# A mixture of experts reads its rows in quarters: 32x32 block transposes on VectorE in place of TensorE's, down weights four neighbouring rows to a partition, gate and up weights at a step of four

## What is computed

```python
def hier_moe(x, norm_g, w_rg, w_re, w_gate, w_up, w_down):
    u = rms_norm(x, norm_g)
    ...
    expert_id = g_sel * EXPERTS_PER_GROUP + top_i
    dense_w = jnp.sum(jax.nn.one_hot(expert_id, N_EXPERTS, dtype=jnp.float32) * gate[..., None], axis=-2)
    h = jax.nn.silu(jnp.einsum('ntd,edf->ntef', u, w_gate)) * jnp.einsum('ntd,edf->ntef', u, w_up)
    h = h * dense_w[..., None].astype(h.dtype)
    return jnp.einsum('ntef,efd->ntd', h, w_down)
```

## Time and profile before

| | |
|---|---|
| median of 3 runs | 1395.42 us (1392.59 to 1399.41) |
| profiled execution | 1393.3 us, its span 1391.3 us |
| PE busy | 1283.8 us, 92% |
| PEld busy | 975.2 us, 70% |
| DVE busy | 516.1 us, 37% |
| ACT busy | 308.4 us, 22% |
| POOL busy | 168.5 us, 12% |
| mean TensorE clock granted | 0.949 of full |
| moved by DMA | 437.00 MB, mean 314 GB/s |

### The profile page before, as it was taken

The page is one execution under the profiler, slowest core; times in us unless marked ns, Lnnn a source line. Parts: engine busy times, 40 slices in busy tenths (PEclk is TensorE's granted clock), DMA queues, the critical chain, the costliest instruction groups (busy, mean ns, idle before and its releaser), DMA issues.

```text
span 1391.3 us, 36243 instructions
## 1 busy us (share of the span) xinstructions
PE 1283.8 (92%) x15268; PEld 975.2 (70%) x15268; DVE 516.1 (37%) x1323; ACT 308.4 (22%) x767; POOL 168.5 (12%) x202
## 2 busy tenths in 40 slices
PE   5979999999986999999999898999997899999996
PEld 5869999999634766667675454545445899999983
DVE  3640000000176545564647566663026200000005
ACT  2200011111142131314144453534101011111000
POOL 4110000010202021212122111210000000000003
PEclk9869999999997999999999899999987899999999
DMA  8959999999898879897979898984264699999976
GB/s 283 369 183 372 382 391 388 393 399 363 295 362 285 278 249 364 274 384 260 384 256 356 263 359 261 345 301 182 93 255 149 245 384 390 391 389 389 390 295 212
DMA packets 147222, 437.00 MB, mean 314 GB/s; under 512 B 20711, under 2 KB 51304, under 8 KB 138270
## 3 DMA queue, kind: packets, MB, share of 16 engines
q1 hardware_dynamic: 99494, 367.58, 71.2%
q10 hardware_dynamic: 37296, 38.09, 8.4%
q0 software_dynamic: 10320, 29.79, 6.7%
HBM read 406.32 MB, written 29.44 MB: 313 GB/s over the span
## 4 chain that ended last, share of the span: by engine, by line
PE 66%; issue 12%; DVE 8%; ACT 6%; DMA 4%; SPq 2%; ACTq 1%; POOL 1%; DVEq 0%; POOLq 0%
PE PS L1102 12%; PE PS L1106 12%; PE PS L1355 8%; PE PS L1134 6%; PE PS L1492 6%; PE PS L1139 6%; PE PS L1024 3%; PE PS L1395 3%; PE PS L1433 2%; DVE KV L2433 2%; PE PS L1456 1%; PE PS L1016 1%; DVE PS L2483 1%; ACT W L1968 1%; DMA KV<-in_cache_k 1%
## 5 line engine op out<-in xcount | busy, mean ns | idle before, releaser
L1106 PE MATMUL PS<-W,KV 128*32 128x128 f32 x3072 | 345.8, 275 | 0.0
L1102 PE MATMUL PS<-W,KV 128*32 128x384 f32 x3072 | 342.6, 492 | 3.2 <-DVE KV L2054 3.2
L1106 PEld LDWEIGHTS PS<-W,KV 128*32 128x32 f32 x3072 | 338.1, 111 | 2.2
L2294 DVE TENSOR_TENSOR KV<-KV,PS 128x384 f32<-128x384 f32 x32 | 17.7, 554 | 483.2 <-PE PS L1120 426.7
L1355 PE MATMUL PS<-W 128*128 128x256 f32 x768 | 178.8, 387 | 0.7 <-ACT KV L1764 0.7
L1355 PEld LDWEIGHTS PS<-W 128*128 128x128 f32 x768 | 144.6, 193 | 30.3 <-issue 7.9
L1134 PE MATMUL PS<-W,KV 128*32 128x384 f32 x1440 | 162.2, 488 | 0.0
L1139 PE MATMUL PS<-W,KV 128*32 128x256 f32 x960 | 162.2, 327 | 0.0
L2433 DVE STREAM_TRANSPOSE KV<-KV 128x1024 f32<-128x1024 f32 x128 | 155.5, 1229 | 7.3 <-DMA KV<-in_cache_k 7.2
L1102 PEld LDWEIGHTS PS<-W,KV 128*32 128x32 f32 x3072 | 150.9, 110 | 4.5 <-DVE KV L2054 4.1
L1139 PEld LDWEIGHTS PS<-W,KV 128*32 128x32 f32 x960 | 95.6, 109 | 14.4
(11 more groups left out here) (305 smaller groups left out, 1478.8 us busy)
## 6 DMA issues: line engine op xcount, KB each, us to landing
W<-in_w_gate SPq DMA_DIRECT2D x32, 2048.0 KB
W<-in_w_up SPq DMA_DIRECT2D x32, 2048.0 KB, 15.1
W<-in_w_down SPq DMA_DIRECT2D x32, 2048.0 KB, 13.3
KV<-in_cache_k SPq DMA_DIRECT2D x256, 256.0 KB, 5.5
W<-in_cache_v SPq DMA_DIRECT2D x128, 512.0 KB, 8.1
yd<-KV ACTq DMA_DIRECT2D x30, 288.0 KB, 7.6
W<-in_w_kvf SPq DMA_DIRECT2D x4, 2048.0 KB, 18.3
W<-in_w_kvf ACTq DMA_DIRECT2D x8, 1024.0 KB, 7.8
```

The lines of the kernel that those rows point to most:

```text
L1102: pe.matmul(PS[32 * q:32 * q + 32, bank, 0:WIDE], x, w[:, k, 0:WIDE], start=(k == 0), stop=(k == KC - 1), tile_position=(0, 32 * q), skip_ ...
L1106: mm = pe.matmul(PS[CAP:P, bank, P * q:P * q + P], x, w[:, k, WIDE:FF], start=(k == 0 and q == 0), stop=(k == KC - 1), tile_position=(0, C ...
```

## The change

1. XS is also seen as rows of 256 floats (XS4), four to a row. The table IDX becomes 128 x 48: for each group q of 32 rows, partition 32a + i has 4 x (row i of the group) + a. An expert's gather is three indirect DMAs (one per q) of 128 quarter rows of 1 KB.
2. To make this come out right, `in_quarters` writes the normalised rows to XS with each quarter permuted, reading them with a step of eight floats.
3. VectorE transposes the gathered 128 x 768 in blocks of 32 x 32 into XQ[j] and multiplies it by the gains in place, three instructions. There are two such buffers, and VectorE works two experts ahead (`xt(e + 2)` behind `hidden(e)`). Expert 0 is done quarter by quarter (`xt_first`), as its three gathers land. `x_tr` is gone.
4. TensorE's order becomes gate(e), h_tr(e-1), up(e), down(e-1), and up now waits for hidden(e-1) itself (h_ready), because xt_ready no longer implies it.
5. A down weight arrives as one run of 16 KB per partition, its rows 4p to 4p + 3. The hidden columns must then come out by residues, so `product` reads the gate and up weights with a step of four: columns of residue 0, 1, 2 in the wide matmuls, of residue 3 in the narrow ones.

```diff
-            return A["w_down"][l, e].rearrange("(f p) n -> p f n", f=FC)
+            return A["w_down"][l, e].rearrange("(p f) n -> p (f n)", f=FC)
...
+        XS4 = XS.rearrange("r (a f) -> (r a) f", a=4)
+        XQ = [a[:, 0:Q4 * 2 * P] for a in (V8[:, 4, :], V4[:, :])]
+        XTQ = [a.rearrange("p (q k n) -> p q k n", q=Q4, k=KC) for a in XQ]
...
-                    after(pool, sem("xt_tr"), e - 1 + l * NE)
+                    after(pool, sem("xg_read"), e - 1 + l * NE)
...
-                    pool.indirect_dma_start(out=XG[j][0:CAP, :], out_offset=None, in_=XS,
-                                            in_offset=bass.IndirectOffsetOnAxis(ap=idc[0:CAP, j:j + 1], axis=0))\
-                        .then_inc(sem(f"xg_in_{j}"), 16)
+                    for q in range(Q4):
+                        pool.indirect_dma_start(out=XG[j][:, 2 * P * q:2 * P * q + 2 * P], out_offset=None, in_=XS4,
+                                                in_offset=bass.IndirectOffsetOnAxis(ap=idc[:, Q4 * j + q:Q4 * j + q + 1], axis=0))\
+                            .then_inc(sem(f"xg_in_{j}"), 16)
...
-                def x_tr(e, j):
-
-                    k = 8 * e + 16 - 8 * j
-                    pe.wait_ge(sem(f"xg_in_{j}"), k + l * (8 * NE))
-                    after(pe, sem("xt_ready"), e + l * NE)
-                    transposes(XG[j], 0, CAP, KC).then_inc(sem("xt_tr"), 1)
...
-                    w = W[:, slot, :].rearrange("p (k n) -> p k n", k=KC)
+                    w = W[:, slot, :].rearrange("p (k n f) -> p k f n", k=KC, f=FC)
                     for k in range(KC):
                         for q in range(Q4):
-                            x = XT[:, k, 32 * q:32 * q + 32]
-                            pe.matmul(PS[32 * q:32 * q + 32, bank, 0:WIDE], x, w[:, k, 0:WIDE], start=(k == 0),
+                            x = XTQ[j][:, q, k, :]
+                            pe.matmul(PS[32 * q:32 * q + 32, bank, 0:WIDE], x, w[:, k, 0:FC - 1, :], start=(k == 0),
                                       stop=(k == KC - 1), tile_position=(0, 32 * q), skip_group_check=True)
...
-                        product(3, 3 * j + 1, count, "up")
+                        after(pe, sem("h_ready"), e + l * NE)
+                        product(3, 3 * j + 1, count, "up", j)
...
                     halves(e, j, 0)
-                    halves(e, j, 1)
                     if not first:
                         h_tr(e - 1)
-                    x_tr(e + 1, 1 - j)
+                    halves(e, j, 1)
...
+            def in_quarters(t, out):
+
+                r = ROWS[t]
+                return dve.tensor_scalar(out[0:r, :].rearrange("p (a k n) -> p a k n", a=4, k=KC),
+                                         H[0:r, t, :].rearrange("p (a n k) -> p a k n", a=4, k=KC), rs[0:r, t:t + 1], None, ALU.mult)
...
-                dve.tensor_copy(IDX[:, :], PS[:, 7, 2 * P:2 * P + NE]).then_inc(sem("routed"), 1)
+                table = IDX[:, :].rearrange("p (q e) -> p q e", q=Q4)
+                for q in range(Q4):
+                    for a in range(4):
+                        ins = dve.tensor_scalar(table[32 * a:32 * a + 32, q], PS[32 * q:32 * q + 32, 7, 2 * P:2 * P + NE], 4.0, float(a),
+                                                ALU.mult, ALU.add)
+                    ins.then_inc(sem("routed"), 1)
...
-                def xt(e):
-                    dve.wait_ge(sem("xt_tr"), e + 1 + l * NE)
-                    gained(XT, 0, l, CAP).then_inc(sem("xt_ready"), 1)
...
+                def xt(e, j):
+                    dve.wait_ge(sem(f"xg_in_{j}"), 24 * e + 32 - 8 * j + l * (24 * NE - 16 + 16 * j))
+                    after(dve, sem("up_done"), e - 1 + l * NE)
+                    dve.transpose(XQ[j], XG[j][:, 0:Q4 * 2 * P]).then_inc(sem("xg_read"), 1)
+                    dve.wait_ge(sem("xg_read"), e + 1 + l * NE)
+                    x = XQ[j].rearrange("p (q k n) -> p q k n", q=Q4, k=KC)
+                    for q in range(Q4):
+                        g = gains[:, l, :].rearrange("p (k a) -> p k a", a=1).to_broadcast([P, KC, 32])
+                        ins = dve.tensor_tensor(x[:, q], x[:, q], g, ALU.mult)
+                    ins.then_inc(sem("xt_ready"), 1)
```

More of the change, by code:

```diff
@@ L1149, in halves @@
                         after(pe, sem("silu_done"), e + l * NE)
-                        product(2, 3 * j, count, "gate")
+                        product(2, 3 * j, count, "gate", j)
                     else:
-                        product(3, 3 * j + 1, count, "up")
+                        after(pe, sem("h_ready"), e + l * NE)
+                        product(3, 3 * j + 1, count, "up", j)
                 def expert(e, j):
@@ L1182, in down_last @@
                     mm.then_inc(sem("down_done"), 1)
-                x_tr(0, 0)
                 expert(0, 0)
@@ L1207, in moe @@
                             pe.wait_ge(sem(f"g_xg{l}"), 16 * (n + 1))
-                            transposes(XG[0], 0, P, KC).then_inc(sem(f"g_step{l}"), 1)
+                            for k in range(KC):
+                                for a in range(4):
+                                    at = 2 * P * a + 32 * k
+                                    mm = pe.matmul(PS[32 * a:32 * a + 32, k // 4, (k % 4) * P:(k % 4) * P + P], XG[0][:, at:at + 32], ident,
+                                                   start=True, stop=True, tile_position=(0, 32 * a), skip_group_check=True)
+                            mm.then_inc(sem(f"g_step{l}"), 1)
                             pe.wait_ge(sem(f"g_step{l}"), 9 * n + 2)
@@ L2032, in norm @@
                 norm_scale(phase, t)
+                if phase in ("r0", "r1"):
+                    return in_quarters(t, out)
                 if gain is None:
@@ L2302, in moe @@
                 dve.tensor_copy(ONTO[4], PS[0:CAP, 4, FC * CAP:FC * CAP + 64]).then_inc(sem("onto_step"), 1)
-                with dve.Fori(1, NE - 1) as e:
-                    hidden(e)
-                    xt(e + 1)
+                with dve.Fori(1, NE - 3, 2) as e:
+                    for j in range(2):
+                        hidden(e + j)
+                        xt(e + j + 2, 1 - j)
+                hidden(NE - 3)
+                xt(NE - 1, 1)
+                hidden(NE - 2)
                 dve.wait_ge(sem("np_ready"), 1 + l * 1)
```

71 lines of the change are left out of this document (44 added, 27 removed).

## The result

The changed kernel takes 1719.88 us (median of 4 runs, 1716.05 to 1726.23) where the kernel before takes 1394.01 us (1391.37 to 1399.41): 1.234 times as long, 95% interval 1.230 to 1.238. I had forecast 1383 us. The loss, 326 us, is the third rival's, and larger than I had priced it.

The account below looks back on a forecast made before the run. DMA queues, about 18.1 us per expert, were taken as the bound hidden by buffer lead: per stage -10.1 slack, -1.0 idle, +2.9 start, +2.0 loads = -6.2 us; two stages -12.4 us, 1383 us; range 1368 to 1406 us.

Parts of the forecast that it names:

- third rival: Gate and up products: four streams stepping on one read path stretch them; at double time about 1660 us; chance 0.18.
- The strided read: Gate and up weights read at a step of four floats: no cost, judged by a stationary-column load with step eight.
- to spare beside the loads: TensorE's spare time per expert against the DMA queues, 18.1 - 16.5 = 1.6 us, credited against slower products.
- The note's two halves: Skill page on SBUF reads: two hits per 16-byte line are wanted, yet a step up to four fp32 is free.
- x_tr's removal: TensorE in the stages: eight transposes per expert go, 1.06 us each expert, 15.9 us per stage if TensorE-bound.
- TensorE stays the bound: Rival, both stages: 16 KB rows save over 0.5 us per expert, stages give 13.0 us each, 1369 us; chance 0.13.
- By bytes nothing changes: Expert gather as 384 packets of 1 KB: DMA cost unchanged by bytes; 0.1 us per expert taken, 0.9 if per packet.
- the loads get dearer: Rival, DMA in the stages: 1 KB gathers and 16 KB rows cost near upper ends, 1395 to 1418 us; chance 0.24.
- POOL's three gathers: Stage start: expert 0 comes in three gathers instead of one, ahead of gate(0), priced at +0.75 us.
- the last rival: Something taken as covered isn't: up waits for hidden behind a late gather, 2.5 us per expert, 1412 us; chance 0.02.
- The lower clock: Stage start: TensorE's slow 6.9 us falls all on products instead of 4.25 us of it, an estimated +1.3 us.
- The 16 KB rows: Down weight loads in 16 KB rows instead of 4 KB: +0.05 us per expert, possible gain 0.6 us.

Follow-up runs that it names:

- gathers apart: Against quarters alone: from expert 2 on, an expert's three gathers wait for gate, up and down of earlier experts, so they are spaced out; 1383.43 us, ratio 0.9955.
- experiment 4: Against gathers apart: each gather issued half a period to a period earlier (gathers early), 1364.75 us; a probe beside it gathers whole 4 KB rows, 1403.13 us.
- quarters alone: The change without the read at a step of four and without the 16 KB down rows; 1402.88 us, ratio 1.008 to the kernel before.
- gathers early: Against gathers apart: every gather half a period to a period earlier, expert 2's three at once; 1364.75 us, ratio 0.981 to the kernel before.

## Why the prediction was wrong, by its steps

- **The strided read.** This is the step that failed: "so a step costs nothing there, at an element per 1.5 ns; one stream of a product takes one per 0.84 ns", and "that is why I put no cost on it". The row of stationary columns showed that one line per 1.5 ns can be opened, and no more. The product needs a float per 0.84 ns, and at one float per line that is a line per 0.84 ns, which no row showed; measured is a line per 1.77 ns. Both rates stood in my sentence, and the second should have set the cost: a row that is slower than the demand is no evidence of a free ride. By that row itself, at 1.5 ns in place of 0.84, a product would be 9.4 us, and the change a loss of over 200 us.
- **Its rival** had the mechanism wrong, and the size too low. Four streams at one path were blamed; one stream alone is as slow (14.69 us against 7.1). Doubling gave 10.3 us per product and 1660 us; measured were 11.1 us. And its 1.6 us per expert "to spare beside the loads" weren't there to be credited. They didn't fit the forecast's own sum either: 32 times 1.6 is 51 us, where that sum has the two bounds only 2 x 6.8 = 13.6 us apart. From its TensorE-bound 1369 us, doubling gives 1369 + 64 x 5.2 = 1702 us.
- **The note's two halves.** Where the two halves of the note in the Trainium skill's page "SBUF — State Buffer" parted, I left the chance of a slow read at 0.18. Its half on two hits per line was right, its half on the free step wrong.
- **x_tr's removal.** Right in size: the period falls from 17.64 to 16.5 us in the kernels with the gathers apart. Two stages of 13.0 us by my sum; experiment 4 gives 27 us, the case "TensorE stays the bound", 1369 us, against 1364.75. That the two agree is in part luck: from the first gate product to the last down product the stages are 16.9 and 17.8 us shorter, and the rest of that profiled execution is 7 us longer.
- **"By bytes nothing changes"** for the gather, with 0.9 us per expert as the dear end: wrong in sign. By the landing times the quarters save about 18.1 - 16.9 = 1.2 us of DMA time per expert. I had ruled out a gain there, though the kernel's trace had no 1 KB gather. The rival "the loads get dearer" (0.24) had no ground at all.
- **POOL's three gathers** I priced only where they stand ahead of gate(0): +0.75 us. There it was nothing (first gather to gate(0): 81.14 to 88.23 us before, 81.18 to 88.28 after, with the longer table behind it). What I left out is what they do beside a busy TensorE, 1.2 us per expert and 5 us per stage in the quarters alone. "It costs nothing" was said of VectorE's side alone; the last rival (0.02) spoke of covered things and named the wrong one.
- **The row scaling** went from 0.74 to 1.15 us for the last tile, 0.4 us where I took 0.3. **VectorE's** 2.2 us per expert is 0.97 + 1.10 = 2.1 us, hidden as said. **The lower clock** at the start costs the changed kernel nothing, since the read is slower than either clock. In the quarters alone only four rounds are slow (89.73 to 92.30 us), and in the kernel of experiment 4 six (89.40 to 93.24 us), less than the 4.25 us of products before and not the 6.9 us that I had counted. So the term of 1.3 us wasn't there.
- **h_tr's place and up's new wait** cost nothing, as said: in the stages of the changed kernel TensorE waits for `hidden` only once each, 0.70 us at the last expert, as before.
- **The 16 KB rows**: right that the time doesn't move, so they had nothing to pay the step with. The loads became slightly faster with them, where I had put +0.05 us per expert.

In short, by stages of the profiled executions, from the first gate product to the start of the last down product:

| kernel | first stage, us | second stage, us |
|---|---|---|
| before | 280.2 | 281.1 |
| quarters alone | 281.9 | 282.1 |
| gathers apart | 272.4 | 272.8 |
| gathers early | 263.2 | 263.3 |
| the change | 446.7 | 446.7 |

The change bundles a gain of 17 to 18 us per stage (before to gathers early), a loss of 19 us per stage where the gathers stand close together, which the slow products hide, and some 5.7 us in each of 64 products (263.2 to 446.7 us, over 32). Only the last is seen in the final time.

## What to carry to other kernels

Before a moving operand is read with a step, count the floats that it takes from each 16-byte line, and hold the rate of the line against the rate at which the matmul takes columns: here one per line halved every product, two per line cost 6%. A row that shows a slower consumer unharmed proves nothing for a faster one. And when one transfer becomes several from POOL, try them spaced out and look at TensorE's "issue" idles: three close together took back all that the removed transposes gave, and the same three spread over the period, and early enough, made the kernel about 2% faster than before.

## What the runs showed that I had not expected

- A stepped stream's rate doesn't depend on TensorE's clock: 0.69 us per round at a granted 0.50 and 0.68 at 1.00.
- Three gathers of 0.95 us each, 0.3 us apart, stop TensorE's issue for 1.2 us though it waits for none of them. In the kernel of experiment 4 two of them 1.1 us apart (230.50 and 232.55 us) stop nothing. Nor do nine in a row there, 0.3 us apart, which end at 93.4 us, four microseconds into gate(0). These nine are written out and take their indices from the table itself, and TensorE is at its lower clock beside them; the three of the loop take theirs from a copy (idc). Which of this matters is open, so that the distance alone is the cause isn't shown.
- The form of the gather (0.39 of 7 MB) moves the total rate of a core with saturated DMA engines from 392 to 418 GB/s.
